# A weight's low half moved to GpSimd, scores that begin before the last queries, and two buffers for a recurrence's modulation chunks

## The chip, the cores and the metric

The program runs on one core of a Trainium2 chip. The metric is device time in microseconds of one execution; the kernel before was run three times on the chip, and once more under the profiler.

## The reference

Four transformer layers on 256 tokens of width 1024, in float32. Layers 0 and 1 are of one kind: they also carry 256 context tokens (layer 1 only reads them), and mix by a Fourier transform, by attention and by a gated recurrence (chunks of 64 in the reference, both directions). Layers 2 and 3 are of another kind and only attend. Each layer ends in a gated feed-forward, and scale, shift and gate come from a conditioning vector. Cut to what matters here:

```python
def first_block(...):            # layers 0, 1
    for l in range(2):
        mod = silu_c @ w_ada[l] + b_ada[l]
        ux = (rmsnorm(x) * (1 + sc_a) + sh_a) @ w_in[l]      # 1024 x 2304
        fx = fourier_mix(ux[..., 0:256], w_four[l])
        ax, ac = attention_group(ux, uc, ...)                # 8 query, 2 key heads of 64, rope
        rx, rc = hgrn_group(ux, uc, ...)                     # 4 heads, forward and backward
        x = x + g_a * (concatenate([fx, ax, rx]) @ w_out[l])
        x = x + g_f * swiglu(rmsnorm(x) * (1 + sc_f) + sh_f, w_gate[l], w_up[l], w_down[l])

def second_block(...):           # layers 2, 3
    for i in range(2):
        mod = (cond @ ada_w[i] + ada_b[i])[:, None, :]
        h = rmsnorm_2(x, norm_mix[i]) * (1 + sc1) + sh1
        y = windowed_gqa(h, ...) if i == 0 else dilated_attention(h, ...)   # 16 / 24 query heads
        x = x + g1 * y
        h = rmsnorm_2(x, norm_ffn[i]) * (1 + sc2) + sh2
        x = x + g2 * swiglu_2(h, ffn_w_in[i], ffn_w_out[i])
```

## The kernel before, in words

Every engine has its own program, written out by hand in order, and semaphores hold them together. Nothing is scheduled: the order on an engine is the order in its function. All weights stream through SBUF in pieces of 8 KB a partition (`load_plan`): for each layer the chunks of `w_in` (256 columns each, in the order of `win_order`), then of `w_out`, then the feed-forward's. SP issues each load when the slot's last user is done. TensorE works in a split precision: a float32 operand is a rounded high part and a low part (the rest), and each product is three matmuls, high by high, high by low, low by high (`mm3`, all recorded on L923). So every weight piece is first split: ScalarE copies `raw` to `whigh` (L1513), and VectorE subtracts, `wlow = raw - whigh` (L2008, in `split`), in place of `raw`. While chunk n is multiplied, the split of n + 3 is made. So the last chunk of each projection triggers the split of the third `w_out` piece (layers 0 to 2) or of the first feed-forward piece (layer 3).

**Projection.** For each `w_in` chunk and each token tile of 128, 24 matmuls make one bank of PSUM; ScalarE copies it to `U` (L1666, in layers 2 and 3 L1662). Query and key columns are then transposed on TensorE (L937, `head_turns`), ScalarE takes the high part (`QHL`, L1699 or L1705; `KHL`, L1710) and VectorE the low part (L2240, L2248, L2253, `heads_low`). In layers 2 and 3 the queries of a chunk are transposed one chunk later, those of the last chunk after the projection. Six banks go round (`open_bank`); TensorE's table `holder` says whose data a bank holds.

**Attention.** TensorE waits for all queries, all keys, the values and for every bank in `holder`, and then goes through units: `scores(n)` into banks 0 and 1 or 2 and 3, `turns` (the probabilities transposed into banks 4 and 5), `values` into bank 6 or 7. VectorE makes the negated maxima (`maximum`: L2314; L2318 and products with the slopes in layer 2; L2327 in layer 3), the inverse of the sums and the scaling of the probabilities (`invert`, L2341 and L2345, the sum with the sink's term at L2337), and the low part of the transposed ones (L2352). ScalarE makes the exponentials (L1739) and the high part (L1752). In layer 2 a unit is a pair of heads for both tiles; in layer 3 a pair of heads of each of three groups for one tile.

**GpSimd** clamps the gates (L805) and applies gains (L795) at the end of the projections of layers 0 and 1, and makes the recurrence's products within a token (`own_pairs`, L834, L841 and following).

**Recurrence (layers 0 and 1).** Eight steps, four token tiles forward and backward. ScalarE and VectorE make a step's gates (L2403 to L2421), TensorE its decays and products (`prepare`, `read`), VectorE weighs (L2448) and masks (L2463). In between stand modulation chunks of later layers (`ada_plan`, `beside`): a 1 MB piece of the modulation weights is loaded by SP (`ada_load`, L688) and multiplied on TensorE, 16 matmuls a chunk, drained by ScalarE (L1538, L1555). Ten chunks stand in layer 1's recurrence, two each in steps 0 and 4. `ada_place` says in which buffer a chunk lies; all ten use the upper half of `AWH`:

```python
slots = {"start": (0, 1, 2, 3), "projection": (5, 6), "feed_forward": (2, 3, 4)}.get(group[0], (1,))
...
if before:
    sp.wait_ge(*ada_used(*before))       # in ada_load: the buffer's last user is done
```

## Time and profile before

| | |
|---|---|
| time, median of 3 | 1998.52 us (1998.48 to 1999.02) |
| the profiled execution | 1997.01 us |
| its span | 1995.2 us |
| mean granted clock of TensorE | 0.935 of 2.4 GHz |
| TensorE busy | 1780.6 us, 89% of the span |
| VectorE, ScalarE, GpSimd busy | 64%, 42%, 4% |
| DMA | 300 MB, 151 GB/s over the span |

The span is the time between the first and the last instruction of the profiled execution; the time is taken around it and is 1.8 us longer. A busy engine need not be the bound: what counts is which wait ends last at a place. The profile infers a "chain that ended last", followed back from the last instruction through whatever released each step. Times in rows are microseconds from the span's start.

### The profile page before, as it was taken

To read this page: it belongs to the slowest core of one execution; us is meant where nothing else is said; L and a number is where in the kernel's file an instruction comes from. 1 tells how busy PE (TensorE), PEld (TensorE's weight loads), DVE (VectorE), ACT (ScalarE), POOL (GpSimd) and SP (SyncE) were. 2 spreads that over 40 slices of the span, in tenths; PEclk is the share of its full clock that TensorE was granted. 3 is DMA by queue.
4 is the path that set the end of the run, shared out by engine and by line. 5 is a ranking of instruction groups with operands and counts; after the bars stand their busy time and mean duration, and the time that the engine had idled before them with its cause. 6 is when DMAs were issued, how large, how long until landed. Compare 5 with 4: busy or idle time off the path is not lost.

```text
span 1995.2 us, 30906 instructions
## 1 busy us (share of the span) xinstructions
PE 1780.6 (89%) x12242; PEld 1597.2 (80%) x12242; DVE 1284.9 (64%) x2358; ACT 842.5 (42%) x1661; POOL 86.4 (4%) x153
## 2 busy tenths in 40 slices
PE   4899888989999999798679899977899997889997
PEld 3789767888888888687568899866799987779996
DVE  1336777558878566657664788856678885575544
ACT  2523664152222231535551544356544435565432
POOL 0000223100000000001021000000000000000000
PEclk8899998799999999899687999989999999899999
DMA  8452011055547654323233899633289873415653
GB/s 263 162 192 84 27 44 43 1 148 170 177 154 213 184 185 143 99 95 90 80 111 90 240 268 283 233 116 85 83 248 279 265 245 109 124 43 155 184 180 127
DMA packets 359119, 300.35 MB, mean 151 GB/s; under 512 B 8048, under 2 KB 333408, under 8 KB 358720
## 3 DMA queue, kind: packets, MB, share of 16 engines
q1 hardware_dynamic: 357584, 294.22, 48.3%
q0 software_dynamic: 1392, 4.15, 0.9%
q8 instruction: 98, 1.61, 0.3%
q14 instruction: 45, 0.37, 0.1%
HBM read 297.30 MB, written 1.05 MB: 150 GB/s over the span
## 4 chain that ended last, share of the span: by engine, by line
PE 74%; DVE 11%; DMA 6%; ACT 5%; issue 3%; SPq 0%; DVEq 0%; POOL 0%; ACTq 0%; POOLq 0%
PE bank L923 71%; PE bank L937 2%; ACT whigh L1513 2%; DVE wlow L2008 2%; DMA raw<-in_w_up 1%; DMA AWH<-in_ada_w 1%; DMA raw<-in_ffn_w_out 1%; DVE A L2345 1%; DVE ACC L2024 1%; DMA A<-in_w_ada 1%; ACT A L1739 1%; DVE HTL L2101 1%; DVE nmax L2314 1%; DMA X<-in_ctx 0%; DVE A L2463 0%
## 5 line engine op out<-in xcount | busy, mean ns | idle before, releaser
L2008 DVE TENSOR_TENSOR wlow<-raw,whigh 128x2048 fp32r<-128x2048 f32 (+1 forms) x183 | 410.0, 2244 | 327.2 <-ACT whigh L1513 326.3
L1513 ACT ACTIVATE whigh<-raw 128x2048 fp32r<-128x2048 f32 (+1 forms) x183 | 343.0, 1878 | 313.4 <-PE bank L923 114.0
L923 PE MATMUL bank<-HTH,whigh 128*128 128x256 f32 (+1 forms) x1424 | 444.3, 312 | 7.5 <-DVE HTL L2101 7.4
L923 PE MATMUL bank<-HTH,wlow 128*128 128x256 f32 (+1 forms) x1424 | 440.4, 309 | 0.0
L923 PE MATMUL bank<-HTL,whigh 128*128 128x256 f32 (+1 forms) x1424 | 440.1, 309 | 0.0
L923 PE MATMUL bank<-whigh,HTH 128*128 128x256 f32 (+1 forms) x1008 | 296.6, 294 | 22.9 <-DVE HTL L2101 6.4
L923 PE MATMUL bank<-wlow,HTH 128*128 128x256 f32 (+1 forms) x1008 | 292.2, 290 | 0.0
L923 PE MATMUL bank<-whigh,HTL 128*128 128x256 f32 (+1 forms) x1008 | 291.9, 290 | 0.0
L923 PEld LDWEIGHTS bank<-HTH,whigh 128*128 128x128 f32 x1424 | 273.6, 192 | 20.8 <-issue 8.2
L923 PEld LDWEIGHTS bank<-HTH,wlow 128*128 128x128 f32 x1424 | 273.3, 192 | 13.6
L923 PEld LDWEIGHTS bank<-HTL,whigh 128*128 128x128 f32 x1424 | 273.7, 192 | 12.6
L2024 DVE SCALAR_TENSOR_TENSOR ACC<-A,cond,ACC 128x256 f32<-128x256 f32 x546 | 257.3, 484 | 16.5
L923 PEld LDWEIGHTS bank<-whigh,HTH 128*128 128x128 f32 x1008 | 199.6, 198 | 26.3 <-issue 21.9
L923 PEld LDWEIGHTS bank<-wlow,HTH 128*128 128x128 f32 x1008 | 199.5, 198 | 0.6
L923 PEld LDWEIGHTS bank<-whigh,HTL 128*128 128x128 f32 x1008 | 199.2, 198 | 0.6
L923 PE MATMUL bank<-whigh,hidden_high 128*128 128x512 f32 x440 | 173.9, 395 | 1.9 <-DVE wlow L2008 1.9
L923 PE MATMUL bank<-whigh,hidden_low 128*128 128x512 f32 x440 | 171.7, 390 | 0.0
L923 PE MATMUL bank<-wlow,hidden_high 128*128 128x512 f32 x440 | 171.2, 389 | 0.0
L1555 ACT ACTIVATE modc<-bank,biast 128x1 f32<-128x1 f32 (+1 forms) x192 | 39.5, 258 | 249.0 <-PE bank L923 247.3
L2536 DVE TENSOR_TENSOR A<-bank,A 128x256 f32<-128x256 f32 (+1 forms) x88 | 42.9, 488 | 101.1 <-PE bank L923 87.1
L937 PE MATMUL bank<-ident,A 128*128 128x128 f32 x436 | 66.2, 289 | 37.3 <-DVE LFL L2421 9.9
L923 PEld LDWEIGHTS bank<-whigh,hidden_high 128*128 128x128 f32 x440 | 82.7, 188 | 18.5 <-DVE wlow L2008 2.1
(218 smaller groups left out, 2286.8 us busy)
## 6 DMA issues: line engine op xcount, KB each, us to landing
raw<-in_ffn_w_in SPq DMA_DIRECT2D x88, 512.0 KB, 5.3
A<-in_ada_w SPq DMA_DIRECT2D x38, 1024.0 KB, 7.2
A<-in_w_ada SPq DMA_DIRECT2D x32, 1024.0 KB, 5.4
raw<-in_w_gate SPq DMA_DIRECT2D x44, 512.0 KB, 6.7
raw<-in_w_up SPq DMA_DIRECT2D x44, 512.0 KB, 6.5
raw<-in_ffn_w_out SPq DMA_DIRECT2D x20, 1024.0 KB, 5.9
raw<-in_w_in SPq DMA_DIRECT2D x18, 1024.0 KB, 5.7
raw<-in_w_down SPq DMA_DIRECT2D x18, 1024.0 KB, 6.1
```

The costliest lines, as they stand in the source:

```text
L923: return nc.tensor.matmul(out, lhsT, rhs, start=start, stop=stop, skip_group_check=True)
L937: return nc.tensor.transpose(out, in_, ident[0:k, 0:k])
L1513: nc.scalar.activation(parts(loads[n])[0], raw_slot(loads[n]), ACT.Copy).then_inc(*made("split_high", loads[n]))
L1555: last = nc.scalar.activation(modc[:, l, 2 * j + c, 0:nc_], ps[:, 2 * c:2 * c + nc_], ACT.Identity, bias=biast[:, c, row:row + 1])
L1739: last = nc.scalar.activation(probs_of(l, n, e, at, size), ps[:, e, at:at + size], ACT.Exp, scale=1.0 if l < 2 else slopes(HEADS_Q[l])[h], ...
L2008: V.tensor_tensor(low, raw_slot(loads[n]), as_float(high), ALU.subtract).then_inc(*made("split_low", loads[n]))
L2024: last = V.scalar_tensor_tensor(out=a, in0=w[:, k, :], scalar=cond[:, cs[i], k:k + 1], in1=a, op0=ALU.mult, op1=ALU.add)
L2101: last = V.scalar_tensor_tensor(out=HTL[:, c, r], in0=XS[g][:, b, k, :], scalar=modc[:, l, base + c, i:i + 1], in1=as_float(HTH[:, c, r]), ...
L2314: V.tensor_reduce(nm.rearrange("p (e i) -> p e i", e=2), ps.rearrange("p e (i c) -> p e i c", i=nt), AX.X, ALU.max, negate=True).then_inc( ...
L2345: last = V.tensor_scalar(part, part, rinv[:, n % 2, col:col + 1], None, ALU.mult)
L2536: V.tensor_tensor(G[:, f % 2, 0:n], ps[:, 0:n], G[:, f % 2, 0:n], ALU.mult) \
```

## The change

Three things, and one that follows from the second.

1. The low half of the piece whose split is due at the last chunk of each layer's projection is made by GpSimd (`low_sem` gives it a semaphore of its own). In layers 0 and 1 it stands behind the clamps and gains and ahead of the recurrence's products. The high half stays with ScalarE; in layers 2 and 3 it moves into the attention, behind the first late query copy.
2. In layers 2 and 3 the queries of the two last chunks (`late_queries`) are transposed within the attention, into banks 7 and 6: the first behind `scores(0)`, the second behind `scores(1)`; ScalarE's and VectorE's parts move alike. Layer 3's chunks come in the order 0, 2, 4, 1, 3, 5, so that the late ones, 3 and 5, are first needed by unit 4.
3. The modulation chunks of layer 1's recurrence use two buffers in turn. The second lies in `U`, in columns of the context tiles that layer 1 does not compute, and is loaded in four pieces.
4. TensorE no longer waits for all banks ahead of attention: `free` waits for each bank where it is first written.

```diff
 def win_order(layer):
-    return (..., (4, 5, 0, 1, 2, 3), (6, 7, 8, 0, 1, 2, 3, 4, 5))[layer]
+    return (..., (4, 5, 0, 1, 2, 3), (6, 7, 8, 0, 2, 4, 1, 3, 5))[layer]
+def late_queries(layer):
+    return win_order(layer)[-2:] if layer >= 2 else ()
+def queries_of(layer, p):
+    return [p // 2] if layer == 2 else [(4 * g + p) // 2 for g in range(GROUPS3)]
 def turns_after(layer, j, n):
-    if n == 1 and at > first_q:
-        out.append(("queries", j - 1))
+    if n == 1 and at > first_q and win_order(layer)[at - 1] not in late_queries(layer):
+        out.append(("queries", win_order(layer)[at - 1]))
 def ada_place(l, j):
-            slots = {...}.get(group[0], (1,))
+            slots = {..., 1: (1, 7)}.get(group[0], (1,))
 def ada_part(w, k):
+            if w is None:
+                a = (0, 256, 512, OFF_HQ)[k % 4]
+                return U[:, 2 + k // 4, a:a + 256]
 def ada_load(l, j):
+                elif slot == 7:
+                    for half in range(2):
+                        for a, k, n in ((0, 0, 3), (OFF_HQ, 3, 1)):
+                            sp.dma_start(U[:, 2 + half, a:a + 256 * n].rearrange("p (k c) -> p k c", k=n),
+                                         src[:, 4 * half + k:4 * half + k + n]).then_inc(*made(f"ada_weights{slot}", l, j, by=16))
 # GpSimd
+            def split(n):
+                pool.wait_ge(*upto("split_high", loads[n]))
+                high, low = parts(loads[n])
+                nc.gpsimd.tensor_tensor(low, raw_slot(loads[n]), high.bitcast(F32), ALU.subtract).then_inc(...)
                 if l < 2:
                     clamped(l)
                     gained(l)
+                    split(index["win", l, win_order(l)[-1]] + HIGH)
                     own_pairs(l)
+                else:
+                    split(index["win", l, win_order(l)[-1]] + HIGH)
 # TensorE
 def open_bank(*key):
+                elif key[0] == "qT_late":
+                    b = NBANKS + 1 - late_queries(key[1]).index(key[2])
 def attention(l):
-                for b in list(holder):
-                    pe.wait_ge(*drained(*holder.pop(b)))
+                def free(*bs):
+                    for b in bs:
+                        if b in holder:
+                            pe.wait_ge(*drained(*holder.pop(b)))
                 def scores(n):
+                    free(2 * (n % 2), 2 * (n % 2) + 1)
+                    for part in queries_of(l, p) if l >= 2 else ():
+                        if part in late_queries(l):
+                            pe.wait_ge(*drained("qT_late", l, part))
                 scores(0)
                 for n in range(len(units) + 3):
+                    if n < 2 and l >= 2:
+                        head_turns(l, "queries", late_queries(l)[n])
                     if 2 <= n < len(units) + 2:
                         turns(n - 2)
 # ScalarE
 def attention(l):
                 for n in range(len(units) + 4):
+                    if n < 2 and l >= 2:
+                        head_turns(l, "queries", late_queries(l)[n])
+                        if n == 0:
+                            split(index["win", l, win_order(l)[-1]] + HIGH)
                     ...
                     if n < len(units):
                         probs(n)
 # VectorE
 def project(l):
                 for at, j in enumerate(win_order(l)):
-                    split(index[("win", l, j)] + HIGH)
+                    if at < len(col_groups(l)) - 1:
+                        split(index[("win", l, j)] + HIGH)
 def attention(l):
                     if n < len(units):
                         maximum(n)
+                    if n < 2 and l >= 2:
+                        heads_low(l, "queries", late_queries(l)[n])
                     if 1 <= n <= len(units):
                         invert(n - 1)
```

How the instructions stand on the engines shows it at three places. First TensorE, where layer 2's projection ends and its attention begins (L937 in the one and L970 in the other are transposes, L923 and L956 matmuls; `DISTR` and `EYE` put the distances into the scores). Before:

```order
L923 MATMUL bank<-whigh,HTL 128x256
L937 MATMUL bank<-ident,A_52 128x128 [waits drained_act,drained_dve]
L937 MATMUL bank<-ident,A_52 128x128 x3
L937 MATMUL bank<-ident,A_52 128x128 [waits drained_act]
L937 MATMUL bank<-ident,A_52 128x128 x3
L923 MATMUL bank<-DISTR,EYE 128x512 [waits eye_set,drained_dve,dist_in,drained_act,values_low]
```

And now:

```order
L956 MATMUL bank<-whigh,HTL 128x256
L956 MATMUL bank<-DISTR,EYE 128x512 [waits dist_in,values_low,eye_set,drained_dve,drained_act]
L956 MATMUL bank<-DISTR,EYE 128x512
L956 MATMUL bank<-KHL_102,QHL_98 128x256 x12
L970 MATMUL bank<-ident,A_52 128x128 [waits drained_act]
L970 MATMUL bank<-ident,A_52 128x128 x3
L956 MATMUL bank<-DISTR,EYE 128x512 [waits drained_dve,drained_act]
```

Both groups of transposes of late queries have moved behind scores. Second, ScalarE at the same place (`U` and the probabilities are shown as A; the copies of the last chunk, a query copy, the split, a query copy, the table load and the first exponentials). Before:

```order
L1662 ACTIVATE A_52<-bank 128x64 x8
L1699 ACTIVATE QHL_98<-bank 128x512
L1513 ACTIVATE whigh<-raw 128x2048
L1699 ACTIVATE QHL_98<-bank 128x512
L1739 ACT_TABLE_LOAD
L1739 ACTIVATE A_53,lsum<-bank,nmax 128x256 x4
```

And now:

```order
L1707 ACTIVATE A_52<-bank 128x64 x8
L1743 ACTIVATE QHL_98<-bank 128x512
L1558 ACTIVATE whigh<-raw 128x2048
L1783 ACT_TABLE_LOAD
L1783 ACTIVATE A_53,lsum<-bank,nmax 128x256 x4
L1789 ACTIVATE sinke<-sinke 128x4
L1743 ACTIVATE QHL_98<-bank 128x512
```

The second query copy now stands behind the first exponentials; the first copy and the split stand where they stood, but wait for transposes that come behind the scores. Third, SP's loads of modulation chunks in layer 1's recurrence (ten in a row before, `L688 DMA AWH<-in_ada_w 128x8x256 x10`). The first three now:

```order
L705 DMA AWH<-in_ada_w 128x8x256
L709 DMA A_52<-in_ada_w 128x3x256
L709 DMA A_52<-in_ada_w 128x256
L709 DMA A_52<-in_ada_w 128x3x256
L709 DMA A_52<-in_ada_w 128x256
L705 DMA AWH<-in_ada_w 128x8x256
```

Every second chunk goes to `U` (A_52), in four pieces; the order of the chunks is the same.

## Rows read from the trace of the kernel before

**Rows 1.** The profile's page, part 4: share of the last chain by engine.

```profile
PE 74%; DVE 11%; DMA 6%; ACT 5%; issue 3%; SPq 0%; DVEq 0%; POOL 0%; ACTq 0%; POOLq 0%
```

**Rows 2.** Chain that ended last, layer 0, 207:219. Columns: start, length in us, what.

```profile
209.21 1.91 ACT whigh L1513
...
215.39 1.66 PE bank L923 x6
```

**Rows 3.** Chain, layer 1, 926:938.

```profile
928.87 2.31 DVE wlow L2008
```

**Rows 4.** TensorE's timeline, layers 2 and 3. Columns: start, length, instruction, idle before.

```profile
1370.80 1.19 PE L923 MATMUL bank<-DISTR,EYE 128*128 128x512 f32 x2 [6.09 <-DVE QHL L2240]
...
1731.22 1.19 PE L923 MATMUL bank<-DISTR,EYE 128*128 128x512 f32 x2 [5.55 <-DVE QHL L2240]
```

**Rows 5.** Chain, layer 1's recurrence and after it.

```profile
977.65 5.33 DMA AWH<-in_ada_w
...
985.08 6.59 DMA AWH<-in_ada_w
...
1019.52 5.49 DMA AWH<-in_ada_w
...
1051.44 18.95 PE bank L923 x112
```

**Rows 6.** Groups of GpSimd instructions by form. Columns: form, count, busy us, mean ns, idle.

```profile
L834 POOL TENSOR_TENSOR A<-A,A 128x256 f32<-128x256 f32 x12 | 8.8, 737 | 125.4 <-DVE A L2419 69.0 <-ACT A L1816 53.3 <-ACT ACC L1538 3.1
...
L841 POOL TENSOR_TENSOR A<-A 128x128 f32<-128x128 f32 x12 | 5.8, 486 | 0.9
```

**Rows 7.** GpSimd's timeline, layer 1's end of projection.

```profile
929.08 3.44 POOL L805 TENSOR_SCALAR A<-A 128x512 f32<-128x512 f32 x1
...
932.50 1.47 POOL L805 TENSOR_SCALAR A<-A 128x512 f32<-128x512 f32 x1
```

**Rows 8.** VectorE's timeline, layer 1's recurrence.

```profile
1014.45 0.28 DVE L2448 TENSOR_TENSOR A<-A 128x128 f32<-128x128 f32 x1
...
1015.27 0.81 DVE L2448 TENSOR_TENSOR A<-A 128x128 f32<-128x128 f32 x1
```

**Rows 9.** GpSimd's timeline, layer 1's recurrence.

```profile
1015.16 0.77 POOL L814 TENSOR_TENSOR A<-HW,A 128x256 f32<-128x256 f32 x1
```

**Rows 10.** VectorE's timeline, first scaling or inversion of layers 0 to 3.

```profile
220.02 0.88 DVE L2345 TENSOR_SCALAR A<-A,rinv 128x512 f32<-128x512 f32 x2
...
936.67 0.89 DVE L2345 TENSOR_SCALAR A<-A,rinv 128x512 f32<-128x512 f32 x2
...
1377.75 0.16 DVE L2337 TENSOR_TENSOR lsum<-lsum,sinke 128x4 f32<-128x4 f32 x1
...
1739.36 0.15 DVE L2339 TENSOR_REDUCE rinv<-lsum 128x2 f32<-128x6 f32 x1
```

**Rows 11.** Windows, layer 1: us; busy PE, PEld, DVE, ACT, POOL; granted clock; DMA.

```profile
946.00:949.00 3.00, 3.00 (x26) 2.67 (x26) 2.96 (x6) 2.02 (x6) 0.00 (x0) 1.00 0.00 0
```

**Rows 12.** ScalarE's timeline, layers 0 and 2.

```profile
211.01 0.41 ACT L1555 ACTIVATE modc<-bank,biast 128x2 f32<-128x2 f32 x2
...
1367.00 1.28 ACT L1739 ACT_TABLE_LOAD   x1
...
1375.34 0.47 ACT L1739 ACTIVATE A<-bank,nmax 128x256 f32<-128x256 f32 x1 [7.05 <-DVE nmax L2321]
```

**Rows 13.** VectorE's timeline, step 6's gate.

```profile
1022.50 0.42 DVE L2421 TENSOR_TENSOR LFL<-A,LFH 128x256 fp32r<-128x256 f32 x1
```

**Rows 14.** TensorE's timeline, step 6's transposes.

```profile
1027.80 0.67 PE L937 MATMUL bank<-ident,A 128*128 128x128 f32 x2
```

**Rows 15.** Busy time and granted clock in stretches of layer 1, columns as in group 11.

```profile
1003.00:1006.00 3.00, 3.00 (x9) 2.32 (x8) 0.00 (x0) 1.97 (x5) 0.00 (x0) 0.50 0.95 317
1072.00:1075.00 3.00, 3.00 (x15) 3.00 (x16) 2.62 (x12) 0.00 (x0) 0.00 (x0) 0.50 0.00 0
1075.00:1078.00 3.00, 3.00 (x26) 3.00 (x26) 1.95 (x6) 0.00 (x0) 0.00 (x0) 0.99 0.00 0
```

More of the change, by code:

```diff
@@ L149, in win_order @@
 def win_order(layer):
-    return ((0, 3, 1, 2, 4, 5, 6, 7, 8), (0, 3, 1, 2, 4, 5, 6, 7, 8), (4, 5, 0, 1, 2, 3), (6, 7, 8, 0, 1, 2, 3, 4, 5))[layer]
+    return ((0, 3, 1, 2, 4, 5, 6, 7, 8), (0, 3, 1, 2, 4, 5, 6, 7, 8), (4, 5, 0, 1, 2, 3), (6, 7, 8, 0, 2, 4, 1, 3, 5))[layer]
 def cols_of(layer, t, a, b):
@@ L598, in parts, with low_sem @@
             return whigh[:, n % HIGH, 0:load_size(key)], wlow[:, n % RAW, 0:load_size(key)]
+        def low_sem(key):
+            return "split_low_pool" if key in [loads[index["win", l, win_order(l)[-1]] + HIGH] for l in range(4)] else "split_low"
         def last_use(key):
@@ L630, in ada_place @@
             members = [c for c in ada_chunks if ada_group(ada_spot[c]) == group]
-            slots = {"start": (0, 1, 2, 3), "projection": (5, 6), "feed_forward": (2, 3, 4)}.get(group[0], (1,))
+            slots = {"start": (0, 1, 2, 3), "projection": (5, 6), "feed_forward": (2, 3, 4), 1: (1, 7)}.get(group[0], (1,))
             n = members.index((l, j))
             slot = slots[n % len(slots)]
-            where = AWH[:, slot] if slot < 2 else AWX[slot - 2] if slot < 5 else AWU[slot - 5]
+            where = AWH[:, slot] if slot < 2 else AWX[slot - 2] if slot < 5 else AWU[slot - 5] if slot < 7 else None
             return slot, where, members[n - len(slots)] if n >= len(slots) else None
         def ada_part(w, k):
+            if w is None:
+                a = (0, 256, 512, OFF_HQ)[k % 4]
+                return U[:, 2 + k // 4, a:a + 256]
             return w[:, k, :] if len(w.shape) == 3 else w[:, k // 4, k % 4, :]
@@ L786, in _ @@
             nc.gpsimd.memset(ones[:, :], 1.0).then_inc(*made("ones_set"))
+            def split(n):
+                pool.wait_ge(*upto("split_high", loads[n]))
+                high, low = parts(loads[n])
+                nc.gpsimd.tensor_tensor(low, raw_slot(loads[n]), high.bitcast(F32), ALU.subtract).then_inc(*made("split_low_pool", loads[n]))
             def gained(l):
@@ L932, in need_parts @@
             def need_parts(key):
-                pe.wait_ge(*upto("split_low", key))
+                pe.wait_ge(*upto(low_sem(key), key))
             def turn(out, in_):
@@ L1077, in project @@
                 modulation_end()
-                if l >= 2:
-                    head_turns(l, "queries", DH * HEADS_Q[l] // 256 - 1)
             def need_u(l, t, a, b):
@@ L1116, in head_turns @@
                 if kind == "queries":
-                    ps = open_bank("qT", l, which)
+                    ps = open_bank("qT_late" if which in late_queries(l) else "qT", l, which)
                     for t in X_TILES:
@@ L1123, in head_turns @@
                             last = turn(ps[:, N * i + P * t:N * i + P * t + P], U[:, t, c:c + P])
-                    last.then_inc(*made("product", "qT", l, which))
+                    last.then_inc(*made("product", "qT_late" if which in late_queries(l) else "qT", l, which))
                     return
@@ L1141, in attention @@
                 for q in query_parts(l):
-                    pe.wait_ge(*drained("qT", l, q))
+                    if q not in late_queries(l):
+                        pe.wait_ge(*drained("qT", l, q))
                 for t in tiles_of(l, "mix"):
@@ L1189, in turns @@
                     for b in range(TURNED):
+                        free(4 + b)
                         if n:
@@ L1203, in values @@
                         pe.wait_ge(*upto("attended", l, before))
+                    free(6 + g % 2)
                     w = 256 * nt
@@ L1229, in attention @@
                     pe.wait_ge(*upto("attended", l, g))
+                free(*list(holder))
             def recurrence(l):
@@ L1671, in project @@
                             head_turns(l, *turns)
-                    split(index[("win", l, j)] + HIGH)
+                    if l < 2 or at < len(col_groups(l)) - 1:
+                        split(index[("win", l, j)] + HIGH)
                     late(("win", l, j))
@@ L1682, in project @@
                 modulation_end()
-                if l >= 2:
-                    head_turns(l, "queries", DH * HEADS_Q[l] // 256 - 1)
             def fourier(l, g):
@@ L1697, in head_turns @@
                 if kind == "queries":
-                    ps = take("qT", l, which)
+                    ps = take("qT_late" if which in late_queries(l) else "qT", l, which)
                     nc.scalar.activation(QHL[l][:, 0, 2 * which:2 * which + 2, :], ps[:, :].rearrange("p (k c) -> p k c", k=2), ACT.Copy) \
@@ L2153, in project @@
                 for at, j in enumerate(win_order(l)):
-                    split(index[("win", l, j)] + HIGH)
+                    if at < len(col_groups(l)) - 1:
+                        split(index[("win", l, j)] + HIGH)
                     if l < 2:
@@ L2174, in project @@
                     heads_low(l, "tile", 3)
-                else:
-                    heads_low(l, "queries", DH * HEADS_Q[l] // 256 - 1)
             def project_out(l, jobs):
@@ L2239, in heads_low @@
                     dve.wait_ge(*upto("q_high", l, which))
-                    V.tensor_tensor(QHL[l][:, 1, 2 * which:2 * which + 2, :], psum("qT", l, which)[:, :].rearrange("p (k c) -> p k c", k=2),
+                    name = "qT_late" if which in late_queries(l) else "qT"
+                    V.tensor_tensor(QHL[l][:, 1, 2 * which:2 * which + 2, :], psum(name, l, which)[:, :].rearrange("p (k c) -> p k c", k=2),
                                     as_float(QHL[l][:, 0, 2 * which:2 * which + 2, :]), ALU.subtract) \
-                        .then_inc(*made("drained_dve", "qT", l, which))
+                        .then_inc(*made("drained_dve", name, l, which))
                     return
```

## The prediction

> **What bounds the kernel now.** I read the last chain first, by engine: TensorE holds 74% of it, VectorE 11%, DMA 6%, ScalarE 5% [rows 1]. So time can be won only where the chain leaves TensorE. I then read the chain in order of time around the places that the diff touches, and the engines' own timelines there.
>
> Four of them are the step from projection to attention. In layer 0 the last projection work on TensorE ends at 209.2; the chain goes through the weight split on ScalarE (1.91), its low half on VectorE and two small low halves, and reaches the scores at 215.39 [rows 2]. Layer 1 is alike, behind a low half of 2.31 [rows 3]. In layers 2 and 3 TensorE stands for 6.09 and 5.55 us until the low halves of the last two query chunks are there, which are themselves queued behind a weight's low half [rows 4]. Then it begins at half speed: two 512-column matmuls in 1.19 [rows 4].
>
> The fifth place is layer 1's recurrence. Four times the chain is a modulation chunk's DMA, 5.3 to 6.6 us; three of the four stand in [rows 5]. All ten chunks go through one buffer: a load is issued when the matmuls on the chunk before are done, and lands too late for the next. The matmuls start where the DMA ends: 983.0, 991.7, 1025.0.
>
> **1. The low half moves to GpSimd.** VectorE loses one 2.3 us instruction at the end of each layer's projection, GpSimd gains one. What it costs there no row shows. GpSimd's two-input instructions take 486 ns for 128 columns and 737 ns for 256 [rows 6], 1.96 ns a column, so 2048 columns would be 0.49 + 1920 x 1.96 ns = 4.2 us. Bounds: VectorE's 2.3 from below, eight times 737 ns, 5.9, from above. I take 4.3. Its readers are far off: the third out-projection chunk in layers 0 to 2, the first feed-forward chunk in layer 3. In layers 0 and 1 the recurrence's own pairs are queued behind it on GpSimd; those waited for VectorE and ScalarE anyway, 122 us in two waits [rows 6]. So the instruction is hidden, but not what it does to VectorE.
>
> That is in the trace too. While VectorE's low half ran from 928.87 [rows 3], a GpSimd instruction that else takes 1.47 us took 3.44 [rows 7]. The other way round, a VectorE product with both inputs in SBUF took 0.81 instead of 0.28 [rows 8] and ended within 0.15 us of the GpSimd instruction beside it [rows 9]. Whichever comes second waits for the whole of the first. Attention has two kinds on VectorE that this may touch: the two-input products on the maxima of layers 2 and 3, and the scaling of the probabilities, two of 512 columns in 0.88 [rows 10]. For the scaling no row shows a clash: the range is from no wait to all that is left of the 4.3. I take the full wait, as the nearest row, the held product, shows.
> The Trainium skill says it more widely (SBUF — State Buffer, "Who interferes with whom"): the pair of ports is an exclusive lock, also against single-input instructions in a two-port mode. By it the four attentions give what is worked out below; were the scaling free, they would give some 6 us more.
>
> **2. The four attentions: the move, the late queries and the waits by bank together.** VectorE is the busiest engine in these loops (2.96 of 3.00 us [rows 11]), so I follow its first scaling.
> - Layer 0. The key and query parts are ready early, but bank 0, which the first scores write, holds a modulation column that ScalarE copies behind its split, until 211.4 [rows 12]. Scores 211.5 to 212.5, maxima to 215.0, scaling possible at 215.8. GpSimd is at the low half from 212.9 to 217.2. Scaling 217.2 instead of 220.02 [rows 10]: **2.8**.
> - Layer 1. The last key part follows ScalarE's copy (end 927.05) instead of the low half: scores 927.9, exponentials 930.2, scaling 932.0 instead of 936.67 [rows 10], 4.7. But GpSimd's clamps run to about 933.4 and its low half from 935 to 939.3, beside a loop whose scaling comes every 3.4 us. At least one is held, for 1.8 (low half starts just behind one) to 4.3 (just ahead). I take 3.5 with the clamps: **1.2**.
> - Layer 2. Scores at 1363.3 instead of 1370.80. ScalarE now does a query copy (0.6), the split (1.9) and a table load (1.3) behind them, ahead of the first exponentials: 1369.3 instead of 1375.34 [rows 12]. The second late copy follows those, and its low half stands ahead of the first inversion: 1372.6 instead of 1377.75 [rows 10], 5.1. GpSimd, at work from 1368.0 to 1372.3, holds the product on the second maxima, about 1 more: **4.2**.
> - Layer 3. Bank 0 holds the last tile's product, copied at 1724.9; scores then, instead of 1731.22. Onward 2.0 (scores), 1.2 (transposes and copy), 1.9, 1.3, 2.4 (exponentials), 0.6 and 0.7 make 1735.0, with GpSimd's hold 1735.4, against 1739.36 [rows 10]: **4.0**. The new chunk order has the same transposes and equal loads.
>
> **3. Two buffers in the recurrence.** SP issues five loads as before and five in four pieces, in a queue with nothing else until the recurrence ends. Chunks 0 and 1 are both there by about 974, so chunk 1's matmuls start at 977.3 instead of 983.0: 5.7. ScalarE and VectorE, idle in that wait, bring the next gates 5.6 earlier. Chunk 2 is issued at 977.65 as chunk 1 was, lands at 983.0 and is used then instead of at 991.7: 8.7 in all. Chunk 3, issued near 979.5, lands near 987; TensorE asks for it at 988.4 instead of 999.2: 10.7. Chunk 4 never waited. Chunk 6 now follows 5 at once instead of at 1025.0. What is late next is VectorE's gate part at 1022.5 to 1022.9 [rows 13], which lets TensorE on 4.9 ahead of 1027.80 [rows 14], then the weighing that ends at 1027.1: 5.5. Sum **16.2**. If the transfers of chunks 2 and 3 share the engines evenly, chunk 2 lands up to 2 later, and so on down: not under 12.
>
> **4. The clock.** At 1003 to 1006 TensorE is busy throughout at a granted 0.50 [rows 15]: 3 us that take 1.5 at 2.4 GHz. With the gaps ahead gone it should be back before this. I take **1.5**, between 0 and 3. Later 18.95 us of chain run at 0.50 [rows 5, 15]; I leave that to a rival, since no row says why it fell there.
>
> **Sum**: 2.8 + 1.2 + 4.2 + 4.0 + 16.2 + 1.5 = 29.9. The profiled execution took 1997.0 us, 1.5 under the median of 1998.5; against the median the forecast is 1998.5 - 30 = **1968.5**. Later stages start earlier by that much and stay as long, since weight loads are issued as slots are used.
>
> **Rivals.**
> - No hold: the scaling passes GpSimd unhindered. For it: the scaling at 936.67 took a usual 0.89 just behind a GpSimd instruction [rows 10]; against: rows 7 to 9. Layer 0 then gives 4.4, layer 1 4.7, layers 2 and 3 9.5: sum 36.3, **1962**.
> - The clock stays up in the recurrence's last part: the 18.95 become some 10.3, 8.6 more: **1960**.
> - The loads collide: 12 from the recurrence, no clock gain, layer 1 nothing: 20, **1978**.
> - Earlier scores only wait for what is late next (exponentials behind ScalarE's split, landings), or the change does not do what it says. The lists of instructions show the moves, so little speaks for it: **1997**.
> - Slower: TensorE's clock stays down through layer 1's out-projection and into its feed-forward. At 0.50, 15 solid matmuls fit in 3 us, at 0.99 26 [rows 15], 0.085 us each; to eat the 30 us and 4 more takes 400 of them, 46 us of solid work. Against it: the clock was back 3 us after solid work began [rows 15]. **2003**.
>
> **How the numbers follow.** Forecast 0.55, no hold 0.15, clock 0.12, colliding loads 0.12, nothing 0.03, slower 0.03. A measurement here tells about 0.2%, 4 us, from no change: faster 0.94, same 0.03, slower 0.03. The range takes in the first four cases with their bounds: down to 1957 (a gain of 41: no hold and half of the late clock), up to 1981 (17: colliding loads and the longest holds).
>
> **What the changed profile would show.** Right: TensorE at the scores within 2.5 us of the last projection matmul in all four layers; one GpSimd instruction of about 4.3 us in each; a scaling held to its end in layers 0 and 1; waits for AWH gone but for chunk 2; the recurrence 16 us shorter. Wrong: no hold (then over 35), a GpSimd low half over 6 us, chunk 3's matmuls waiting for DMA, or an attention loop that starts 5 us earlier and ends no earlier.

## The result and the profile after

| | before | after |
|---|---|---|
| median of 3 | 1998.52 us | 1969.89 us (1968.27 to 1971.40) |
| ratio of the times | 1 | 0.9856, 95% interval 0.9833 to 0.9878 |
| the profiled execution, its span | 1997.01, 1995.2 us | 1968.27, 1966.5 us |
| mean granted clock | 0.935 | 0.946 |

The change wins 28.6 us, against a forecast of 1968.5 and a range of 1957 to 1981. The later kernels ran in three groups, each on a chip of its own (experiments 1 to 4; 5, 6, 10 and the first run of 7; 8, 9, 11 and the second run of 7). Executions of one kernel lie further apart there (the kernel before from 1990.4 to 2007.2 us in the 17 executions of the first group); so they are compared as ratios to the kernel before beside them, and by their traces. One execution of the changed kernel in experiment 5 took 2911.5 us at a mean granted clock of 0.553, in the slow state, and stands in no ratio.

The view that I began with before is of no use now. Part 4 of the changed kernel's page reads:

```profile
PE 18%; issue 14%; DVE 5%; DMA 5%; ACT 2%; SPq 0%; POOL 0%; DVEq 0%; ACTq 0%; POOLq 0%
```

These shares add to 44%; before they filled the span [rows 1]. The inferred chain breaks off on its way back, and for the windows around 210 and 930 us it has no row. So I read the engines' timelines, and for the ledger the start of the same matmul in both traces: before minus after is what has been gained up to there. Between two places:

| stretch | forecast | profile after | second profile of it |
|---|---|---|---|
| start and layer 0's projection | - | -1.9 | -0.5 |
| layer 0, attention to feed-forward | 2.8 | 0.1 | 0.0 |
| layer 1, attention | 1.2 | -2.5 | -2.5 |
| layer 1's recurrence, up to its last step | 16.2 + 1.5 | 17.0 | 15.9 |
| its last step and the next projection's begin | rival, 8.6 | 8.9 | 6.8 |
| up to layer 2's attention | - | -2.8 | 0.0 |
| layer 2, into attention | 4.2 | 5.4 | 5.7 |
| between | - | 1.4 | 1.5 |
| layer 3, into attention | 4.0 | 3.1 | 3.1 |
| sum | 29.9 | 28.7 | 30.0 |

(The rival's 8.6 is outside the forecast's sum.) The sum came out right with two terms wrong: layers 0 and 1 gave 6.4 less than forecast, and the late clock gave 8.9 that only a rival held. Another 3.3 were lost in the three stretches that have no forecast (-1.9, -2.8 and 1.4); in the second profile these give 1.0 together, so they differ between executions of one program. The place of each, in rows.

**Begin of the scores**, TensorE's timeline of the changed kernel, layers 0 to 3 (columns as in rows 4):

```profile
213.57 2.93 PE L956 MATMUL bank<-KHL,QHL 64*128 64x512 f32 x12 [2.43 <-ACT modc L1600]
...
929.79 1.66 PE L956 MATMUL bank<-KHL,QHL 64*128 64x512 f32 x12 [1.40 <-DVE KHL L2301]
...
1344.52 0.70 PE L956 MATMUL bank<-DISTR,EYE 128*128 128x512 f32 x2
...
1699.58 0.70 PE L956 MATMUL bank<-DISTR,EYE 128*128 128x512 f32 x2 [0.86 <-ACT A L1707]
```

The idle of 6.09 and 5.55 [rows 4] is gone or 0.86, and the two matmuls take 0.70 instead of 1.19: the clock was not lost ahead of them. Layer 0 waits for the modulation column in bank 0, as forecast.

**The hold in layers 0 and 1.** VectorE's timeline (first fence) and GpSimd's (second), changed kernel; these rows answer to [rows 7, 10] (L833 is a clamp, L823 a gain, L814 the low half):

```profile
218.19 1.76 DVE L2393 TENSOR_SCALAR A<-A,rinv 128x512 f32<-128x512 f32 x2
...
936.47 5.62 DVE L2393 TENSOR_SCALAR A<-A,rinv 128x512 f32<-128x512 f32 x2
```

```profile
214.74 4.53 POOL L814 TENSOR_TENSOR wlow<-raw,whigh 128x2048 fp32r<-128x2048 f32 x1
...
929.45 6.11 POOL L833 TENSOR_SCALAR A<-A 128x512 f32<-128x512 f32 x4
935.54 1.40 POOL L823 TENSOR_TENSOR A<-A 128x256 f32<-128x256 f32 x2
936.91 4.50 POOL L814 TENSOR_TENSOR wlow<-raw,whigh 128x2048 fp32r<-128x2048 f32 x1
```

Two scalings take 0.88 when alone. In layer 1 the pair takes 5.62, 4.74 more, and ends 0.7 behind the low half. It began at 936.47, ahead of the low half and beside the second gain product, and so waited through the end of the one and the whole of the other: 4.74 is more than the low half's 4.50. In layer 0 it is 0.88 more: the low half had begun earlier and was nearly through. The probabilities' transposes wait for the pair and for the low part behind it (PTA), and TensorE stands for 4.87:

```profile
942.84 1.94 PE L970 MATMUL bank<-ident,A 128*128 128x128 f32 x8 [4.87 <-DVE PTA L2400]
```

The same eight took 1.17 before at 940.46. The row's 1.94 is at the lower clock: the granted clock reads 0.56 from 943 to 948.

**Layers 2 and 3.** VectorE, GpSimd and TensorE, changed kernel, one fence each:

```profile
1349.81 4.01 DVE L2367 TENSOR_TENSOR nmax<-nmax,steep 128x4 f32<-128x4 f32 x1
...
1704.97 4.17 DVE L2376 TENSOR_TENSOR gmax<-gmax,steep 128x8 f32<-128x8 f32 x1
```

```profile
1349.28 4.51 POOL L814 TENSOR_TENSOR wlow<-raw,whigh 128x2048 fp32r<-128x2048 f32 x1 [59.18 <-ACT whigh L1558]
...
1704.61 4.50 POOL L814 TENSOR_TENSOR wlow<-raw,whigh 128x2048 fp32r<-128x2048 f32 x1 [350.81 <-ACT whigh L1558]
```

```profile
1352.43 0.73 PE L956 MATMUL bank<-DISTR,EYE 128*128 128x512 f32 x2 [3.78 <-ACT A L1783]
```

A product of four columns takes 4.01 us instead of 0.16, and ends within 0.1 of GpSimd's instruction. Yet it costs only about 1 us: ScalarE is at the first exponentials until 1352.3 anyway, and waited 1.09 and 0.69 for the held maxima. TensorE's 3.78 in the last fence is a wait for those first exponentials.

**The recurrence.** TensorE's timeline and its waits from 960 to 1062 (columns of the second: who waited for whom, us in total, times, longest):

```profile
987.84 1.54 PE L956 MATMUL bank<-AWH,cond 128*32 128x256 f32 x16 [3.63 <-DMA AWH<-in_ada_w]
```

```profile
PE bank L956 <- DMA AWH<-in_ada_w: 3.6, 1, 3.6
```

One wait for a chunk is left, and it is chunk 2's, as forecast.

**The clock**, windows of the changed kernel, columns as in rows 11:

```profile
1003.00:1006.00 3.00, 2.99 (x18) 2.35 (x18) 2.92 (x13) 2.52 (x6) 2.53 (x7) 1.00 0.68 238
1052.00:1055.00 3.00, 3.00 (x28) 3.00 (x27) 2.61 (x13) 0.00 (x0) 0.00 (x0) 1.00 0.00 0
```

Against [rows 15]: 18 matmuls in the first three microseconds instead of 9, and where the next projection begins 28 instead of 15. The granted clock is 1.00 in both.

GpSimd's groups, columns as in rows 6:

```profile
L814 POOL TENSOR_TENSOR wlow<-raw,whigh 128x2048 fp32r<-128x2048 f32 x4 | 18.0, 4511 | 410.0 <-ACT whigh L1558 410.0
L833 POOL TENSOR_SCALAR A<-A 128x512 f32<-128x512 f32 x8 | 12.0, 1523 | 0.1
```

The low half takes 4.51 us; I had taken 4.3 from narrower forms.

### The profile page after: what moved, and what is told of

Same layout as the page of the kernel before. It is cut to its first block and busy times, and to the rows that moved or that the text cites. A ratio compares the mean times of both kernels' runs of the same rounds, so it can differ in the third digit from the quotient of the medians.

```text
span 1966.5 us, 30929 instructions
## 1 busy us (share of the span) xinstructions
PE 1769.9 (90%) x12242; PEld 1590.2 (81%) x12242; DVE 1288.9 (66%) x2354; ACT 840.8 (43%) x1661; POOL 99.4 (5%) x157
## 5 line engine op out<-in xcount | busy, mean ns | idle before, releaser
L2056 DVE TENSOR_TENSOR wlow<-raw,whigh 128x2048 fp32r<-128x2048 f32 (+1 forms) x179 | 400.6, 2241 | 302.7 <-ACT whigh L1558 302.1
L956 PE MATMUL bank<-HTH,whigh 128*128 128x256 f32 (+1 forms) x1424 | 444.0, 312 | 8.4 <-DVE HTL L2149 7.8
L956 PE MATMUL bank<-HTH,wlow 128*128 128x256 f32 (+1 forms) x1424 | 440.3, 309 | 0.0
L956 PE MATMUL bank<-HTL,whigh 128*128 128x256 f32 (+1 forms) x1424 | 440.0, 309 | 0.0
L956 PE MATMUL bank<-whigh,HTH 128*128 128x256 f32 (+1 forms) x1008 | 297.7, 295 | 22.1 <-DVE HTL L2263 6.3
L956 PE MATMUL bank<-wlow,HTH 128*128 128x256 f32 (+1 forms) x1008 | 293.3, 291 | 0.0
L956 PE MATMUL bank<-whigh,HTL 128*128 128x256 f32 (+1 forms) x1008 | 292.8, 291 | 0.0
L956 PEld LDWEIGHTS bank<-HTH,whigh 128*128 128x128 f32 x1424 | 273.1, 192 | 21.7 <-issue 8.4
L956 PEld LDWEIGHTS bank<-HTH,wlow 128*128 128x128 f32 x1424 | 273.0, 192 | 13.4
L956 PEld LDWEIGHTS bank<-HTL,whigh 128*128 128x128 f32 x1424 | 273.2, 192 | 12.7
L2072 DVE SCALAR_TENSOR_TENSOR ACC<-A,cond,ACC 128x256 f32<-128x256 f32 x546 | 257.3, 484 | 16.5
L956 PEld LDWEIGHTS bank<-whigh,HTH 128*128 128x128 f32 x1008 | 200.3, 199 | 25.4 <-issue 20.8
L956 PEld LDWEIGHTS bank<-wlow,HTH 128*128 128x128 f32 x1008 | 200.4, 199 | 0.7
L956 PEld LDWEIGHTS bank<-whigh,HTL 128*128 128x128 f32 x1008 | 200.1, 199 | 0.8
L956 PE MATMUL bank<-whigh,hidden_high 128*128 128x512 f32 x440 | 174.0, 396 | 2.4 <-DVE wlow L2056 2.4
L956 PE MATMUL bank<-whigh,hidden_low 128*128 128x512 f32 x440 | 171.8, 390 | 0.0
L956 PE MATMUL bank<-wlow,hidden_high 128*128 128x512 f32 x440 | 171.4, 389 | 0.0
L970 PE MATMUL bank<-ident,A 128*128 128x128 f32 x436 | 67.7, 294 | 41.6 <-DVE LFL L2471 11.9
L956 PEld LDWEIGHTS bank<-whigh,hidden_high 128*128 128x128 f32 x440 | 82.7, 188 | 19.0 <-DVE wlow L2056 2.7
```

What stands on the lines that cost most here:

```text
L956: return nc.tensor.matmul(out, lhsT, rhs, start=start, stop=stop, skip_group_check=True)
L970: return nc.tensor.transpose(out, in_, ident[0:k, 0:k])
L2056: V.tensor_tensor(low, raw_slot(loads[n]), as_float(high), ALU.subtract).then_inc(*made("split_low", loads[n]))
L2072: last = V.scalar_tensor_tensor(out=a, in0=w[:, k, :], scalar=cond[:, cs[i], k:k + 1], in1=a, op0=ALU.mult, op1=ALU.add)
```

## The experiments

What I thought after the first profile: (a) whichever of VectorE and GpSimd begins second waits for the other's whole instruction, which is what layer 1 lost; (b) the recurrence's gain is the two buffers' alone; (c) the late clock is a consequence of these buffers. Rivals stand in the expectations. All ratios are to the kernel before, with 95% intervals.

**1. The two buffers alone**, on the kernel before.

```diff
-            slots = {...}.get(group[0], (1,))
+            slots = {..., 1: (1, 7)}.get(group[0], (1,))
...
+                elif slot == 7:
```

> Kernel before with the two buffers alone. Theory: the recurrence's gain in the changed kernel, 25.5 us by the same matmuls in both traces, needs nothing else of the change: 16 us of waits for AWH and some 9 us of clock, since TensorE no longer pauses there. Then 1998.5 - 25.5 = 1973 us, with one wait for AWH left (about 3.6 us) and no 24 us at a granted 0.50 at the recurrence's end. Rival A: the clock's part came from the earlier start of the attention; then only 16 to 18 us, 1981 to 1982. Rival B: the loads, in a layer 1 that starts elsewhere, collide: 1986.

Ratio 0.9907 (0.9876 to 0.9938), some 19 us. In its trace the recurrence gains 15.2 up to its last step and 8.5 behind that, 23.7 together, with one wait for AWH (2.2 us); the rest of the program stood 7.7 us behind the trace of before in stretches that it doesn't change. So (b) holds: nothing else of the change is needed. The median, 1981.3 us, lies where rival A had put it (1981 to 1982), and speaks for less than 25.5; the trace has the late clock that rival A leaves out. Experiment 7 bears on that.

**2. GpSimd's low half alone**, on the kernel before.

```diff
                     gained(l)
+                    split(index["win", l, win_order(l)[-1]] + HIGH)
                     own_pairs(l)
```

> Kernel before with the low halves on GpSimd alone (all banks are still waited for, the queries stay ahead of attention). Theory of the port's hold: layer 0 gains 0 to 1 us, layer 1 loses about 2.5 (a scaling held for over 4 us), layers 2 and 3 gain 2 to 2.5 each, as their scores come 3 us earlier but a product on the maxima is held until GpSimd ends: 1998.5 - 2.5 = 1996 us. Rival, no hold by GpSimd (what was late in layer 1 was something else of the change): every layer gains 2.3 to 4: 1986 to 1988.

Ratio 0.998 (0.9957 to 1.0002), as expected. The profiled execution, 1988.2 us, is one of the fastest of twelve (median 1996.3). By its trace layer 0 gains 3.8, layer 1's attention ends 3.7 later, and layers 2 and 3 gain about 3 each. The hold is longer than one instruction. VectorE, then GpSimd, around layer 1's first scaling:

```profile
926.56 7.71 DVE L2359 TENSOR_SCALAR A<-A,rinv 128x512 f32<-128x512 f32 x2
```

```profile
926.60 1.56 POOL L815 TENSOR_SCALAR A<-A 128x512 f32<-128x512 f32 x1
928.13 1.40 POOL L805 TENSOR_TENSOR A<-A 128x256 f32<-128x256 f32 x2
929.50 4.48 POOL L796 TENSOR_TENSOR wlow<-raw,whigh 128x2048 fp32r<-128x2048 f32 x1
```

The first of the pair takes 1.13. The second begins at 927.62 and takes 6.65: it waits through the end of a clamp (L815), two gain products and the low half, which GpSimd ran without a pause between them, and ends at 934.27, 0.3 behind the last.

**3. The low half in eight pieces.**

```diff
-                nc.gpsimd.tensor_tensor(low, raw_slot(loads[n]), high.bitcast(F32), ALU.subtract).then_inc(...)
+                for a in range(0, 2048, 256):
+                    part = nc.gpsimd.tensor_tensor(low[:, a:a + 256], raw[:, a:a + 256], high[:, a:a + 256]..., ALU.subtract)
+                part.then_inc(...)
```

> Changed kernel, GpSimd's low half cut into eight instructions of 256 columns (0.74 us each by the nearest rows, 6 us together). Theory: VectorE waits for the GpSimd instruction that is running, and for no more than that one. Then no VectorE instruction there is held for over 0.8 us, layer 1's second scaling ends 4 us earlier, layers 0, 2 and 3 gain 0.9, 1.1 and 0.7: 6.7 us, 1963 us. Rival A: VectorE gives way at each piece, so the eight waits add up to 3 us a layer and half of the gain is lost: 1966. Rival B: the hold lasts until GpSimd's whole queue of pieces is done: 1971 to 1972, a scaling of 6 us again.

Ratio 0.9828 (0.98 to 0.9857), against 0.9846 (0.982 to 0.9873) for the changed kernel in experiment 5: 3.6 us better in the middle, inside the intervals, where 6.7 were expected. The traces say more. Layer 1's attention now gains 2.9 instead of losing 2.5. VectorE in layers 0 and 1, then GpSimd in layer 0:

```profile
219.29 2.36 DVE L2396 TENSOR_SCALAR A<-A,rinv 128x512 f32<-128x512 f32 x1
...
941.40 1.54 DVE L2396 TENSOR_SCALAR A<-A,rinv 128x512 f32<-128x512 f32 x2
```

```profile
218.59 2.78 POOL L816 TENSOR_TENSOR wlow<-raw,whigh 128x256 fp32r<-128x256 f32 x4
```

In layer 1 a scaling waits for what is left of one piece, and pieces wait for scalings in turn (the eight take 6.30 us there, 5.52 in layer 0). In layer 0 one scaling took 2.36: it began 0.02 behind a piece and was let in only when that and the last two were through, and by the attention's end nothing was gained there (0.0 against 2.4 for the changed kernel). So neither the theory nor rival B holds alone: a piece is the usual hold, a row of pieces can be one.

**4. The low half behind the recurrence's own products** (layers 0 and 1).

```diff
-                    split(index["win", l, win_order(l)[-1]] + HIGH)
                     own_pairs(l)
+                    split(index["win", l, win_order(l)[-1]] + HIGH)
```

> Changed kernel, in layers 0 and 1 GpSimd's low half behind the recurrence's own products instead of ahead of them (layers 2 and 3 as changed). Theory: the cost goes with the instruction. Layer 1's attention gains 5, layer 0's 1, and at each recurrence's end VectorE's weighing (14 products in 3.9 us) is held for up to 4.5 us, on the chain: between 1964 (half of each hold hidden) and 1970 (none). The trace must show a VectorE product of over 3 us there. Rival: no hold there, only scalings are sensitive: 1963.5.

Ratio 0.9854 (0.9829 to 0.9879), 1972.5 us. The cost went with the instruction. VectorE, then GpSimd, at the recurrence's end:

```profile
1031.88 8.21 DVE L2498 TENSOR_TENSOR A<-HW,A 128x128 f32<-128x128 f32 x14
```

```profile
1033.18 4.54 POOL L814 TENSOR_TENSOR wlow<-raw,whigh 128x2048 fp32r<-128x2048 f32 x1
```

Fourteen products take 8.21; in the changed kernel's profile they take 3.88. Layer 1's attention loses nothing to it (a gain of 3.9), and the recurrence gains 16.5 instead of 25.9. Of these 9.4 us, 3.9 go at the held product. The rest is missing behind it, where the granted clock from 1033 to 1056 reads 0.53, against 0.93 in the changed kernel; the second run of experiment 7 and experiments 8 and 9 lack it there without any hold, so it is not shown to be the hold's. The rival (only scalings are held) falls.

**5. The changed kernel again, and 6. the low half put where VectorE reads PSUM.** In layers 2 and 3 experiment 6 also cuts the low half in eight. They ran beside each other on one chip; the edit of 6:

```diff
-                    split(index["win", l, win_order(l)[-1]] + HIGH)
                     own_pairs(l)
+                    pool.wait_ge(*upto("scanned", l, 6))
+                    split(index["win", l, win_order(l)[-1]] + HIGH)
                 else:
-                    split(...)
+                    split(..., 256)
```

> The changed kernel once more, as it is, beside the next three on the same chip: about 0.985 of the kernel before. In its trace the held instructions should stand again where they stood (a scaling held for over 4 us in layer 1, products on the maxima of over 3.5 us in layers 2 and 3), since the order fixes them; what the clock gives in the two recurrences may differ by some us from the first profile.

> Changed kernel; in layers 0 and 1 GpSimd's low half waits until VectorE has done its last weighing products and the read-out behind them (the next work there takes PSUM, 5 and 12 us of it); in layers 2 and 3 it is cut in eight. Theory: the hold needs a VectorE instruction with both inputs, or its only one, in SBUF. Then nothing is held in the recurrences, layer 1's attention gains 5 us and layer 0's 1 against the changed kernel, layers 2 and 3 together 0.6: 6.5 us below the changed kernel run beside it, ratio to the kernel before about 0.982. Rival A: masks and read-outs from PSUM are held as well: a mask of 3 to 4.5 us in the traces and half of the gain gone. Rival B: the clock takes the gain back, as in layer 0 of the first profile: below 2 us.

Ratios 0.9846 (0.982 to 0.9873) and 0.9815 (0.9786 to 0.9845), a difference of 6.2 us, near the 6.5 expected, though the intervals overlap. By the spans of the profiles it is 1.6 us against the second profile of the changed kernel and 3.3 against the first, since the late clock gave only 3.1 here. The second profile of the changed kernel has the holds again (a pair of scalings of 5.64, products of 4.00 and 4.17). In the other, VectorE and GpSimd at the recurrence's end:

```profile
1032.12 0.44 DVE L2517 COPY_PREDICATED A<-tb_masks,bank 128x256 f32<-128x256 uint8 x1 [0.71 <-ACT A L1915]
```

```profile
1031.49 4.52 POOL L816 TENSOR_TENSOR wlow<-raw,whigh 128x2048 fp32r<-128x2048 f32 x1 [2.99 <-DVE A L2540]
```

A mask whose data come from PSUM takes its usual 0.44 beside GpSimd: rival A falls. Layer 1's attention gains 3.9 here. Layer 0 kept its gain too, 3.3; why it can is read at the end.

**7. The low half back on VectorE**, run twice, on two chips. GpSimd's two calls of `split` go, and on VectorE:

```diff
-                    if at < len(col_groups(l)) - 1:
+                    if l < 2 or at < len(col_groups(l)) - 1:
                         split(index[("win", l, j)] + HIGH)
...
                         heads_low(l, "queries", late_queries(l)[n])
+                        if n:
+                            split(index["win", l, win_order(l)[-1]] + HIGH)
```

> Changed kernel with the low half back on VectorE: in layers 0 and 1 at the end of the projection as before, in layers 2 and 3 behind the second late low half. Theory: the move to GpSimd is worth little by itself: 3 in layer 0, minus 2.5 in layer 1, 1 each in layers 2 and 3. So 2 to 3 us slower than the changed kernel beside it. Rival: the move is what makes the four attentions begin earlier, and undoing it loses 8 us or more.

> The changed kernel with all low halves back on VectorE, once more. Its first profile showed 1963.5 us of span, as fast as the changed kernel, but its timed executions went from 1965 to 1986 with a median of 1979. Theory: the scatter is of the clock, and the profiled one was by chance the fastest; the move is worth 2 to 3 us: ratio to the kernel before 0.986 to 0.988. Rival: the median stands (0.9896), and the move of the low half is worth about 10 us in most executions, somewhere that a fast execution does not show; then this trace, if it is a slow one, has a stretch with over 8 us more than the changed kernel's.

Ratios 0.9896 (0.9868 to 0.9924) and 0.9875 (0.9852 to 0.9898). The same program was profiled at 1963.5 and at 1972.5 us of span, and the two traces differ at one place above all: the 23 us at the recurrence's end. The same window of the first and of the second profile:

```profile
1033.00:1056.00 23.00, 19.58 (x177) 17.74 (x178) 14.41 (x43) 3.76 (x11) 1.46 (x2) 0.93 0.00 1
```

```profile
1033.00:1056.00 23.00, 21.54 (x125) 18.78 (x126) 11.44 (x34) 3.76 (x11) 0.85 (x2) 0.50 0.00 1
```

177 matmuls at a granted 0.93, 125 at 0.50. Against the trace of before this stretch gained 8.6 in the one and lost 0.1 in the other. So (c) falls: with one buffer no profile has the high clock there, but with two the same program can have it or not. Of the ten profiles of this study with two buffers and no hold at that place, five gained 6.8 to 8.9 there (both of the changed kernel, experiments 1 and 3, the first of this one) and five only -0.1 to 3.1 (the second of this one, experiments 6, 8, 9 and 11). Four of these last five are all the profiles of the third chip, and the two profiles of this program come from two chips: whether the chip or the single execution decides is not separated here.

**8. and 9. Where the move to GpSimd pays**: the low half on VectorE in layers 0 and 1 only, and in layers 2 and 3 only (each half of the diff of 7).

> Changed kernel with the low half on VectorE at the end of the projection in layers 0 and 1 only. By the traces: 3 us lost in layer 0's attention, 2.5 won in layer 1's: the same as the changed kernel within 1 us, ratio 0.985. Rival: if most of the 10 us sits here, 0.989.

> Changed kernel with the low half on VectorE in layers 2 and 3 only, behind the second late low half. By the trace of the kernel with all four on VectorE, layer 2's passage gains 4.6 instead of 5.4 us, layer 3's loses 0.6 instead of gaining 3.1: 4.5 us slower than the changed kernel, ratio 0.987. Rival: the move is worth nothing here, 0.985.

Ratios 0.9867 (0.9844 to 0.9889) and 0.9876 (0.9853 to 0.9898). By the traces: in layers 0 and 1 next to nothing is gained or lost up to the end of the two attentions (0.3 and 0.0), against 2.4 and -2.5 in the changed kernel. In layers 2 and 3 the passages gain 4.6 and lose 0.7, against 5.4 and 3.1. So by the traces the move is worth next to nothing in the first two layers together and 4.6 us in the last two, most of it in layer 3. The ratios make it 4 and 6 us, and 6 and 10 us for all four (experiment 7's two), all against experiment 5, which for 8, 9 and the second of 7 ran on another chip, and each with intervals of about 5 us to either side. That they lie above the traces in all four cases stays open.

**10. One buffer.**

```diff
-            slots = {..., 1: (1, 7)}.get(group[0], (1,))
+            slots = {...}.get(group[0], (1,))
```

> Changed kernel with one buffer in layer 1's recurrence. Theory: the recurrence takes 24 us more (17 of waits and early clock, 7 of late clock), as the kernel with the two buffers alone gained: 24 us above the changed kernel beside it, ratio to the kernel before about 0.997, with 24 us at a granted 0.50 at the recurrence's end. Rival: 16 to 18 us, if the late clock is a matter of where the recurrence starts.

Ratio 0.9956 (0.994 to 0.9973), 1993.0 us: 22.4 above the changed kernel beside it. The waits from 960 to 1085 have the four chunks again, the granted clock from 1051 to 1075 reads 0.51, both as expected, and the recurrence gains nothing (-0.7):

```profile
PE bank L956 <- DMA AWH<-in_ada_w: 16.1, 4, 5.7
```

**11. ScalarE's high half later**, on the kernel of 6.

```diff
                     if n < 2 and l >= 2:
                         head_turns(l, "queries", late_queries(l)[n])
-                        if n == 0:
-                            split(index["win", l, win_order(l)[-1]] + HIGH)
+                    if n == 2 and l >= 2:
+                        split(index["win", l, win_order(l)[-1]] + HIGH)
```

> The kernel gap (GpSimd's low half at the recurrence's end in layers 0 and 1, in eight pieces in layers 2 and 3) and ScalarE's high half of layers 2 and 3 moved behind the exponentials of the second unit, into a wait of 2.1 us for the turned probabilities. Theory: the first exponentials begin 1.9 us earlier in each of the two layers, and the pieces that now run beside the loop hold VectorE for up to 0.7 each, some 1.5 in all: between 1 and 3.5 us below gap, ratio to the kernel before 0.980 to 0.981. Rival: VectorE is the bound of that loop, so the pieces take back everything: 0.9815 or above.

Ratio 0.9789 (0.9766 to 0.9812), 1959.8 us (1953.8 to 1962.2), the best of all: 5.2 us below experiment 6, more than expected, though these intervals overlap too and the two ran on different chips. ScalarE and VectorE in layer 2:

```profile
1344.57 0.47 ACT L1787 ACTIVATE A<-bank,nmax 128x256 f32<-128x256 f32 x1
...
1348.85 1.95 ACT L1562 ACTIVATE whigh<-raw 128x2048 fp32r<-128x2048 f32 x1
1350.65 1.16 ACT L1800 ACTIVATE PTA<-bank 128x512 fp32r<-128x512 f32 x2
```

```profile
1351.31 2.73 DVE L2397 TENSOR_SCALAR A<-A,rinv 128x256 f32<-128x256 f32 x4
```

The high half fills the wait for the turned probabilities. Four scalings beside the pieces take 2.73 instead of 1.14, 1.6 of hold as expected. The passage of layer 2 gains 7.0 against 6.1 in experiment 6, that of layer 3 6.9 against 3.3. By these passages the rival falls.

## Why the prediction came out right, and where it did not

**The sum: nearer than its terms.** Layers 2 and 3 and the recurrence's waits gave what was forecast. That the total came within 1.4 us is luck: without the late clock the same kernel would have taken about 1979 us, still inside the range, but 10 us above the forecast.

**Layers 2 and 3: right, step by step.** Corrected for what had been gained ahead (18.8 and 25.6), the scores begin 7.5 earlier in layer 2 (forecast 7.5), the first exponentials 6.1 (6.0), the inversion 4.2 (4.2); in layer 3 the inversion is 3.9 earlier (4.0). The product on the maxima was the instruction that was held, and about 1 us of it counted.

**The recurrence: right.** Chunks 1, 2 and 3 start 6.0, 8.2 and 10.9 earlier than the layer's attention ended (forecast 5.7, 8.7, 10.7), step 6's transposes 17.3 (17.7 with the clock's 1.5), and the loads did not collide.

**Layer 1: the term was mis-sized.** The first scaling was to come 4.7 earlier and did. The hold was taken at 3.5; it was 4.74 on one pair and 0.36 on the pair before, beside the clamps. The range "1.8 to 4.3" had supposed a low half of 4.3 and one hold only, where two can follow each other and one can outlast the low half. The other 2 us went with the clock: TensorE's granted clock reads 0.71 from 933 to 943 and 0.56 from 943 to 948, around the wait of 4.87; in the trace of before it reads 1.00 from 938 to 948. I had priced the waiting engine, not the engine that waits for it: forecast +1.2, measured -2.5 twice.

**Layer 0: right at its place (2.8 where the first pair of scalings ends, against 2.8), gone later.** Between 288 and 305 us the granted clock reads 0.86 before (first fence) and 0.52 after (second):

```profile
288.00:305.00 17.00, 13.04 (x114) 11.04 (x115) 13.10 (x42) 7.93 (x21) 7.86 (x16) 0.86 0.17 57
```

```profile
288.00:305.00 17.00, 14.99 (x92) 13.41 (x96) 8.29 (x29) 5.46 (x14) 6.73 (x14) 0.52 0.00 0
```

This costs 3.5. It comes back by 340 (0.80 before and 1.00 after from 308 to 325), and 2.4 go again up to 375 (0.59 and 0.56). A layer 0 that is unchanged shows the like: the kernel with the two buffers alone, which leaves layer 0 as it was, has a granted 0.58 from 288 to 305 and loses 3.5 there too. Experiments 6 and 11 have one and the same layer 0 and both gain 3.8 up to its attention's end; with 0.83 in that window the one keeps 3.3 of it, with 0.50 the other keeps nothing. What sets the clock there stays open. The step that failed is "later stages start earlier by that much and stay as long".

**The late clock: a rival at 0.12 that came in five profiles of ten.** The forecast left the 18.95 us at 0.50 as they were, "since no row says why it fell there". One trace of before could not tell a property of the program from one execution's; experiment 7 shows that it varies with the program unchanged, though between two chips. The changed kernel itself has it in both its profiles (8.9 and 6.8), and all its executions but the one of 2911.5, seven in all, lie between 1966.6 and 1972.4 us, so no run shows this kernel without it. That one buffer back costs 22.4 and the two alone win 19, and not 25.9, fits a clock that comes only at times.

**The rivals.** "No hold" is out (experiments 2 to 4), "loads collide" is out, "slower" never showed. Two slips in them change nothing: layer 0 without a hold is 4.2 by the prediction's own times (220.02 less 215.8), not 4.4; and the work from 1051.44 to 1070.39 [rows 5] was at half clock too, so that the clock was back 3 us after solid work began is not what the rows say.
The Trainium skill's rule on the pair of ports (SBUF — State Buffer, "Who interferes with whom") decided that rival, and the traces agree with it: scalings with a single SBUF input were held for 4.7 us, PSUM reads were not. The Trainium skill also says there that the one that comes second waits for the other's whole instruction. The traces show waits that are longer: in experiment 2 one went through the end of a clamp and three instructions behind it.

## What to carry to other kernels

Before an operation moves from VectorE to GpSimd, list what VectorE runs from SBUF beside it: the whole length of the moved instruction can reappear as one wait. Put it where VectorE reads PSUM, which kept 3.8 and 3.9 us here in the attentions of layers 0 and 1, or cut it, which helped in layer 1 and not in layer 0. A stretch at a lower granted clock in one trace need not belong to the program, so both outcomes go into the range.

## What was not expected of the hardware

- A hold lasted for several GpSimd instructions in a row: 6.65 us for one scaling (the end of one instruction and three more), 2.36 for another (three pieces of 0.7). When both engines had been alternating, each waited for one only. What decides between the two was not tried.
- The cost of a hold can be 25 times the held instruction (0.16 us became 4.01), and still 1 us on the path.
- The granted clock at one place of one program was 0.93 and 0.50 in two executions, on two chips, worth 9 us of 1970.
